# Eight wide then eight narrow products in the FFN up stage, and the last value-and-gate unit behind the first sparse head's scores

## The chip, the cores and the metric

The kernel runs on one NeuronCore of one Trainium2 chip. The metric is the device time of one execution in microseconds (us), lower is better. Three runs of the kernel before took 1211.58, 1211.7 and 1215.43 us; the median is 1211.7 us. The profile is of one further execution, of 1215.52 us, whose span from the first to the last instruction is 1213.6 us.

## The reference, cut to what matters

Two blocks are computed one after the other on 256 tokens of width 1024, in fp32. The first has a latent attention, a feed-forward stage (FFN), a differential attention and a second FFN. The second has an FFN, a mixed stage (sparse attention of eight heads beside a gated recurrence of four heads) and a last FFN. Of these the change touches the four FFNs and the mixed stage:

```python
def conv_ffn(x, w_up, conv_w, conv_b, w_down):      # FFN 0 and 1, hidden 2816
    u = x @ w_up
    ...                                             # three taps along the tokens
    g, val = c[..., :FFN_HIDDEN], c[..., FFN_HIDDEN:]
    return (jax.nn.gelu(g) * val) @ w_down

def swiglu(x, w_gu, w_down):                        # FFN 2 and 3, hidden 2752
    gate, up = jnp.split(x @ w_gu, 2, axis=-1)
    return (jax.nn.silu(gate) * up) @ w_down

def hybrid_mixer(h, w_in, ...):
    parts = jnp.split(h @ w_in, IN_SPLITS, axis=-1)
    nq, k_c, v_c, k_s, v_s, k_w, v_w, gl, hq, hf, hi, hg = parts
    o_nsa = nsa_group(nq, k_c, v_c, k_s, v_s, k_w, v_w, gl, ...)
    o_hg = hgrn2_group(hq, hf, hi, hg, lower_bound, hg_norm)
    return jnp.concatenate([o_nsa, o_hg], axis=-1) @ w_out

# the end of hgrn2_group
o = o * lax.rsqrt(jnp.mean(o * o, axis=-1, keepdims=True) + EPS) * out_norm
o = o.reshape(B, S, HG_WIDTH) * jax.nn.silu(g_in)
```

## The kernel before, in words

Each fp32 operand of a large product is split in two: a rounded high part (`hi`, made by ScalarE, named ACT) and the remainder (`lo`, made by VectorE, named DVE). TensorE (PE) then multiplies hi by hi, hi by lo and lo by hi. Weights come in units of 128 x 2048 elements by the SP queue's DMAs into `raw_u`, two slots; ACT writes `hi_u`, DVE `lo_u`, and PE takes a unit when both are done. Nothing schedules by cost: each of the five engines has its own list, written out by hand, and waits on named semaphores where it needs another engine.

An FFN has 22 tiles of 128 hidden columns. For tile t, PE does `up(t)`, and between two of them `down(t-2)`, twelve products of 512 columns (lines 595 to 597). In `up`, for the gate (s = 0) and the value (s = 1) and for each of eight slices k of the input, PE does a pair (`mm_beside`, lines 601 and 602): a wide product of 512 columns with the high weights as stationary operand, against the high and low input side by side, and a narrow product of 256 columns with the low weights against the high input. The narrow one adds into the second half of the same PSUM bank. So a full tile has 16 pairs, wide and narrow in turn. Tiles 2 to 19 are in a hardware loop. The first tile of an FFN goes over k outside and s inside, since it waits for each slice of the input; the last tile of FFN 2 and 3 has only 64 hidden columns and does gate and value in one series of 8 pairs.

In the mixed stage, `mix()`, PE's order around the change is: `values_and_gates(0)` and `(1)`, the four transposes of `c_h`, `values_and_gates(2)`, the small products of the compressed keys and values (lines 1116 and 1120, which end in semaphore `c_kv`), `values_and_gates(3)`, and then the loop over the heads. One `values_and_gates(i)` is one weight unit, `U_HI + i`, with 24 products of 512 columns into PSUM banks 0 to 3; after the fourth, banks 0 and 2 hold the values of the recurrence, which DVE copies to `h_v` (line 2069), and banks 1 and 3 its gates, to which ACT applies SiLU into `h_g` (line 1621); GpSimd (POOL) multiplies these by the norm's gain (line 583). In step i of the head loop PE does `scores(i)` into banks 4 to 7 (lines 1132 to 1136), `level(i-1, 1)` (line 1178), `values(i-2)` (lines 1160 to 1164), `turn(i-1)` (line 1150, into banks 0 and 1) and `level(i, 0)` (line 1178, into bank 3). In step 0 it waits before `level(0, 0)` for `h_ready`, `h_v_out` and `h_g_out`. DVE takes the maxima of the scores (lines 2118 to 2122), ACT the exponentials (line 1638), DVE the reciprocals and the scaling (lines 2104 to 2111), and DVE also takes each level (line 2079) and updates the queries with the decay (lines 2086 and 2094); POOL updates the keys (`hgrn`, lines 541 and 545).

## Time and profile before

| | |
|---|---|
| median of three runs | 1211.7 us (1211.58 to 1215.43) |
| profiled execution | 1215.52 us |
| its span | 1213.6 us |
| mean granted TensorE clock in it | 0.991 |
| PE busy | 1170.0 us (96%), 6627 products |
| DVE busy | 809.6 us (67%) |
| ACT busy | 695.9 us (57%) |
| POOL busy | 66.4 us (5%) |
| HBM read and written | 192.84 MB and 1.05 MB, 160 GB/s over the span |
| chain of waits that ends last | PE 85%, DVE 6%, ACT 4%, DMA 2%, issue 1%, POOL 1%, SP's queue 1% |

"Busy" is the time in which at least one instruction of the engine runs. Products overlap each other in the array: one of 512 columns is shown with about 0.4 us though the next starts after less, so PE's pace is read from the distance of the starts and not from the durations. PEld is the load of a product's stationary operand, which overlaps the product before it. The granted clock of PE is 1.00 at 2.4 GHz and 0.50 at 1.2 GHz.

### The profile page before, as it was taken

Reading aid. Unit: us, or ns where it says so; the run is one execution under the profiler, and the core shown is the slowest. Engines: PE = TensorE matmul, PEld = TensorE weight load, DVE = VectorE, ACT = ScalarE, POOL = GpSimd, SP = SyncE. Lnnn points to the kernel's source line nnn. Section 1 sums busy time; section 2 is a strip of 40 time slices with the busy share of each in tenths; the row PEclk is TensorE's granted clock in tenths of the full one; section 3 lists DMA queues with packets and bytes.
Section 4 is the critical chain, followed back from the end, with each engine's and each line's share of the span. In section 5 each row is a group of like instructions: output and inputs, shape, how many; then the busy total and the mean of one; then the engine's idle time right before and its main releaser. Section 6 shows DMA issues by size and latency. Waiting matters only on the chain.

```text
span 1213.6 us, 19122 instructions
## 1 busy us (share of the span) xinstructions
PE 1170.0 (96%) x6627; PEld 990.7 (82%) x6641; DVE 809.6 (67%) x1169; ACT 695.9 (57%) x1175; POOL 66.4 (5%) x98
## 2 busy tenths in 40 slices
PE   9999999999899989999999999999988999999997
PEld 7976788888799867888886888887887877888885
DVE  5855788887656558888878555556656655665554
ACT  5455666665556547666656554545565545555543
POOL 0201000000200020000002000000000220000000
PEclk9999999999899999999999999999999999999999
DMA  7514666666343436666654666644674015767661
GB/s 225 180 56 125 184 204 191 195 175 203 111 140 132 148 115 179 203 182 203 184 163 139 207 184 181 205 122 131 184 236 139 1 36 168 200 175 201 182 165 60
DMA packets 241056, 194.55 MB, mean 160 GB/s; under 512 B 11214, under 2 KB 223792, under 8 KB 241008
## 3 DMA queue, kind: packets, MB, share of 16 engines
q1 hardware_dynamic: 240928, 193.88, 53.4%
q8 instruction: 30, 0.49, 0.2%
q14 instruction: 18, 0.15, 0.0%
q10 hardware_dynamic: 80, 0.03, 0.0%
HBM read 192.84 MB, written 1.05 MB: 160 GB/s over the span
## 4 chain that ended last, share of the span: by engine, by line
PE 85%; DVE 6%; ACT 4%; DMA 2%; issue 1%; POOL 1%; SPq 1%; POOLq 0%; ACTq 0%; DVEq 0%
PE psum L601 26%; PE psum L602 13%; PE psum L595 12%; PE psum L596 12%; PE psum L597 12%; DVE lo_u L1701 1%; PE psum L1178 1%; DMA raw_u<-in_cmp_v_w 1%; ACT hi_u L1273 1%; ACT hi_u L1276 1%; DVE lo_u L1718 1%; DMA raw_u<-in_diff_w_qkv 1%; PE psum L937 1%; PE psum L1150 1%; DVE normed L1735 1%
## 5 line engine op out<-in xcount | busy, mean ns | idle before, releaser
L601 PE MATMUL psum<-act_hl,hi_u 128*128 128x512 f32 x1392 | 495.9, 399 | 4.5 <-DVE lo_u L1718 3.2
L602 PE MATMUL psum<-act_hl,lo_u 128*128 128x256 f32 x1392 | 390.3, 280 | 0.0
L601 PEld LDWEIGHTS psum<-act_hl,hi_u 128*128 128x128 f32 x1392 | 261.5, 188 | 70.8 <-issue 7.1
L1718 DVE TENSOR_TENSOR lo_u<-raw_u,hi_u 128x2048 fp32r<-128x2048 f32 x109 | 249.8, 2291 | 93.6 <-ACT hi_u L1276 57.5
L602 PEld LDWEIGHTS psum<-act_hl,lo_u 128*128 128x128 f32 x1392 | 262.8, 189 | 3.1
L1346 ACT ACTIVATE arena<-psum 128x256 f32<-128x256 f32 x174 | 66.1, 380 | 166.9 <-PE psum L602 166.8
L1783 DVE TENSOR_TENSOR arena<-psum,arena 128x256 f32<-128x256 f32 x174 | 73.6, 423 | 110.2 <-ACT arena L1346 110.0
L1282 ACT ACTIVATE hi_u<-raw_u 128x2048 fp32r<-128x2048 f32 x72 | 137.3, 1907 | 8.5 <-DMA raw_u<-in_ffn_w_gu 8.5
L595 PE MATMUL psum<-hi_d,hid_hi 128*128 128x512 f32 (+1 forms) x352 | 138.8, 394 | 0.1
L596 PE MATMUL psum<-lo_d,hid_hi 128*128 128x512 f32 (+1 forms) x352 | 137.9, 392 | 0.0
L597 PE MATMUL psum<-hi_d,hid_lo 128*128 128x512 f32 (+1 forms) x352 | 137.0, 389 | 0.0
L1793 DVE SCALAR_TENSOR_TENSOR arena<-arena,vecs 128x255 f32<-128x255 f32 x176 | 85.1, 483 | 42.4 <-ACT arena L1354 31.4
L1723 DVE TENSOR_TENSOR lo_d<-raw_d,hi_d 128x1024 fp32r<-128x1024 f32 x88 | 106.8, 1217 | 8.3 <-ACT hi_d L1291 8.3
L595 PE MATMUL psum<-act_hl,hi_u 128*128 128x256 f32 (+1 forms) x320 | 93.3, 291 | 6.0 <-DVE lo_u L1701 5.6
L1291 ACT ACTIVATE hi_d<-raw_d 128x1024 fp32r<-128x1024 f32 x88 | 91.6, 1045 | 0.0
L596 PE MATMUL psum<-act_hl,hi_u 128*128 128x256 f32 (+1 forms) x320 | 90.9, 284 | 0.0
L597 PE MATMUL psum<-act_hl,lo_u 128*128 128x256 f32 (+1 forms) x320 | 90.9, 284 | 0.0
L1701 DVE TENSOR_TENSOR lo_u<-raw_u,hi_u 128x1024 fp32r<-128x1024 f32 (+4 forms) x62 | 65.5, 1086 | 34.2 <-ACT hi_u L1273 34.0
L1273 ACT ACTIVATE hi_u<-raw_u 128x1024 fp32r<-128x1024 f32 (+4 forms) x62 | 55.7, 944 | 55.8 <-PE psum L597 37.6
L595 PEld LDWEIGHTS psum<-hi_d,hid_hi 128*128 128x128 f32 (+1 forms) x352 | 66.0, 188 | 18.1 <-issue 3.0
L1276 ACT ACTIVATE hi_u<-raw_u 128x2048 fp32r<-128x2048 f32 x37 | 70.6, 1909 | 16.7 <-PE psum L597 12.2
L1354 ACT ACTIVATE arena<-arena,vecs 128x256 f32<-128x256 f32 x88 | 53.0, 602 | 44.8 <-DVE arena L1783 44.1
(249 smaller groups left out, 1673.7 us busy)
## 6 DMA issues: line engine op xcount, KB each, us to landing
raw_u<-in_ffn_w_up SPq DMA_DIRECT2D x88, 512.0 KB, 5.6
raw_d<-in_ffn_w_down SPq DMA_DIRECT2D x86, 512.0 KB, 3.6
raw_u<-in_ffn_w_gu SPq DMA_DIRECT2D x84, 512.0 KB, 5.6
raw_u<-in_diff_w_qkv SPq DMA_DIRECT2D x24, 512.0 KB, 4.6
raw_u<-in_w_in SPq DMA_DIRECT2D x24, 512.0 KB, 4.3
raw_u<-in_mla_w_o SPq DMA_DIRECT2D x8, 512.0 KB, 3.7
raw_u<-in_diff_w_o SPq DMA_DIRECT2D x8, 512.0 KB, 3.7
raw_u<-in_w_out SPq DMA_DIRECT2D x8, 512.0 KB, 4.1
```

Source lines behind the costliest of these rows:

```text
L595: pe.matmul(o, s_hi, m_hi, start=start, stop=False)
L596: pe.matmul(o, s_hi, m_lo, start=False, stop=False)
L597: return pe.matmul(o, s_lo, m_hi, start=False, stop=stop)
L601: pe.matmul(psum[0:n, bank, :], s_hi, m_hl.rearrange("p a t -> p (a t)"), start=start, stop=False)
L602: return pe.matmul(psum[0:n, bank, SEQ:], s_lo, m_hl[:, 0, :], start=False, stop=stop)
L1276: act.activation(unit_view(hi_u, u), unit_view(raw_u, u), ACT.Copy).then_inc(S("hi_u_done"), 1)
L1282: act.activation(u_slot(hi_u, u0), u_slot(raw_u, u0), ACT.Copy).then_inc(S("hi_u_done"), 1)
L1291: act.activation(hi_d[:, d_slot(d) if b is None else d % 2, :], raw_d[:, d % 2, :], ACT.Copy)\
L1701: dve.tensor_tensor(v[0][:, r], v[1][:, r], v[2][:, r].bitcast(F32), ALU.subtract)\
L1718: dve.tensor_tensor(v[0], v[1], v[2].bitcast(F32), ALU.subtract).then_inc(S("lo_u_done"), 1)
L1723: dve.tensor_tensor(lo_d[:, slot, :], raw_d[:, d % 2, :], hi_d[:, slot, :].bitcast(F32), ALU.subtract).then_inc(S("lo_d_done"), 1)
L1793: dve.scalar_tensor_tensor(buf[0:n, slot, o], up_sum[0:n, slot, part, x], vecs[0:n, bass.ds(w, 1)], buf[0:n, slot, o], ALU.mult, ALU.add). ...
```

## The change

Two things change. The helper `up` of the FFN does a tile's products, for gate and value each, as eight wide ones and then eight narrow ones; the first tile and the last narrow tile of FFN 2 and 3 keep the pairs. In the mixed stage one after another of `values_and_gates(1)`, `(2)` and `(3)` moves one place down the list of PE, the last of them behind `scores(0)`; ACT's `split_u(U_HI + 3)` moves behind its copy of `c_ht`; ACT copies the gates out of PSUM in head step 0 and applies SiLU to them in step 8 in one instruction; DVE takes the maxima of head 0 before its split of the next unit and not in the loop; and POOL's product with the gain moves behind `hgrn()`.

```diff
@@ pool @@
+            hgrn()
             gate = h_g.rearrange("p t (h d) -> p (t h) d", h=HGH)
-            pool.wait_ge(S("h_g_out"), 2)
+            pool.wait_ge(S("h_k_upd"), 7)
+            pool.wait_ge(S("h_g_out"), 1)
             pool.tensor_tensor(gate, gate, hgain[:].unsqueeze(1).broadcast_to([P, 8, P]), ALU.mult)\
                 .then_inc(S("h_g_gained"), 1)
-            hgrn()
+            pool.wait_ge(S("h_g_gained"), 1)
             root("hgrn", 0, 0, 8, P, "h_sums", 1).then_inc(S("rstd"), 1)
@@ tensor: ffn, up @@
-                    for s, k in order:
-                        if first and s == 0:
-                            pe.wait_ge(S("act_lo"), 8 * i + k + 1)
-                        hi, lo = views[s]
-                        mm = mm_beside(4 + 2 * slot + s, n, hi[:, k, :], lo[:, k, :], act_hl[:, k],
-                                       k == 0, k == KC - 1)
-                        if k == KC - 1:
-                            mm.then_inc(S("gate_up" if s == 0 else "used_u"), 1)
+                    if first:
...
+                        return
+                    for s, (hi, lo) in enumerate(views):
+                        o = psum[0:n, 4 + 2 * slot + s, :]
+                        for k in range(KC):
+                            pe.matmul(o, hi[:, k, :], act_hl[:, k].rearrange("p a t -> p (a t)"),
+                                      start=k == 0, stop=False)
+                        for k in range(KC):
+                            mm = pe.matmul(o[:, SEQ:], lo[:, k, :], act_hl[:, k, 0, :], start=False, stop=k == KC - 1)
+                        mm.then_inc(S("gate_up" if s == 0 else "used_u"), 1)
@@ tensor: mix @@
                 values_and_gates(0)
-                values_and_gates(1)
...
                 mm.then_inc(S("c_h_tr"), 1)
-                values_and_gates(2)
+                values_and_gates(1)
...
                 mm.then_inc(S("c_kv"), 1)
-                values_and_gates(3)
+                values_and_gates(2)
...
                     if i == 0:
+                        values_and_gates(3)
 
                         pe.wait_ge(S("h_ready"), 1)
                         pe.wait_ge(S("h_v_out"), 2)
-                        pe.wait_ge(S("h_g_out"), 2)
+                        pe.wait_ge(S("h_g_copied"), 2)
@@ scalar: mix @@
                 split_u(U_HI + 2)
-                split_u(U_HI + 3)
                 act.wait_ge(S("c_h_tr"), 1)
                 act.activation(c_ht, psum[:, 4, 0:120].rearrange("p (a b) -> p a b", a=4), ACT.Copy)\
                     .then_inc(S("c_ht_out"), 1)
+                split_u(U_HI + 3)
...
                 split_u(U_HI + 4)
-                for t in range(TT):
-                    act.wait_ge(S("used_u"), U_HI + 4)
-                    act.activation(h_g[:, t, :], psum[:, 1 + 2 * t, :], ACT.Silu).then_inc(S("h_g_out"), 1)
...
+                    if i == 0:
+                        for t in range(TT):
+                            act.wait_ge(S("used_u"), U_HI + 4)
+                            act.activation(h_g[:, t, :], psum[:, 1 + 2 * t, :], ACT.Copy).then_inc(S("h_g_copied"), 1)
+                    if i == H:
+                        act.wait_ge(S("h_g_copied"), 2)
+                        act.activation(h_g, h_g, ACT.Silu).then_inc(S("h_g_out"), 1)
@@ vector: mix @@
+                def maxima(i):
+                    dve.wait_ge(S("n_scores"), i + 1)
...
+                maxima(0)
                 split_u(U_HI + 4)
...
-                    if i < H:
-                        dve.wait_ge(S("n_scores"), i + 1)
...
+                    if 0 < i < H:
+                        maxima(i)
```

On PE, the end of the second tile of an FFN and the start of the looped tiles, before. `L601` is the wide and `L602` the narrow product; `L755` and `L709` are the loop's own instructions.

```order
L602 MATMUL psum<-act_hl,lo_u 128x256
L755 UNCONDITIONAL_BRANCH
L755 ISA
L709 ISA
L601 MATMUL psum<-act_hl,hi_u 128x512
L602 MATMUL psum<-act_hl,lo_u 128x256
L601 MATMUL psum<-act_hl,hi_u 128x512
```

The same place now; `L738` is the wide, `L741` the narrow product, and `L597` is the first of the down products.

```order
L741 MATMUL psum<-act_hl,lo_u 128x256 x8
L767 UNCONDITIONAL_BRANCH
L767 ISA
L711 ISA
L738 MATMUL psum<-act_hl,hi_u 128x512 x8
L741 MATMUL psum<-act_hl,lo_u 128x256 x8
L738 MATMUL psum<-act_hl,hi_u 128x512 x8
L741 MATMUL psum<-act_hl,lo_u 128x256 x8
L747 REGISTER_ALU
L597 MATMUL psum<-hi_d,hid_hi 128x512
```

The number of products is the same; the change between wide and narrow comes four times in a tile and not thirty-two times.

On PE in the mixed stage, the end of `values_and_gates(3)`, `scores(0)` (`L1132` to `L1136`), `level(0, 0)` (`L1178`) and the start of `scores(1)`, before:

```order
L596 MATMUL psum<-lo_u,act_hl 128x512
L597 MATMUL psum<-hi_u,act_hl 128x512
L1132 MATMUL psum<-causal_b,slopes 128x414 x2
L1133 MATMUL psum<-arena 128x143
L1134 MATMUL psum<-arena 128x128
L1135 MATMUL psum<-arena 128x271
L1136 MATMUL psum<-arena 128x256
L1178 MATMUL psum<-arena 128x128 x4
L1132 MATMUL psum<-causal_b,slopes 128x414 x2
```

Now, first the end of `values_and_gates(2)`, `scores(0)` (`L1143` to `L1147`) and the first products of `values_and_gates(3)`:

```order
L598 MATMUL psum<-lo_u,act_hl 128x512
L599 MATMUL psum<-hi_u,act_hl 128x512
L1143 MATMUL psum<-causal_b,slopes 128x414 x2
L1144 MATMUL psum<-arena 128x143
L1145 MATMUL psum<-arena 128x128
L1146 MATMUL psum<-arena 128x271
L1147 MATMUL psum<-arena 128x256
L597 MATMUL psum<-hi_u,act_hl 128x512
L598 MATMUL psum<-lo_u,act_hl 128x512
```

And the end of the unit's 24 products, `level(0, 0)` (`L1189`) and the start of `scores(1)`:

```order
L598 MATMUL psum<-lo_u,act_hl 128x512
L599 MATMUL psum<-hi_u,act_hl 128x512
L1189 MATMUL psum<-arena 128x128 x4
L1143 MATMUL psum<-causal_b,slopes 128x414 x2
L1144 MATMUL psum<-arena 128x143
```

Nothing stands any longer between the unit's last product and `level(0, 0)`, whose waits are for the copies out of the unit's banks.

On ACT between the copies of the compressed keys and values and the exponentials of head 0, before; `L1276` is the split of unit `U_HI + 4`, `L1621` the SiLU of the gates:

```order
L1616 ACTIVATE arena<-psum 15x128
L1276 ACTIVATE hi_u<-raw_u 128x2048
L1621 ACT_TABLE_LOAD
L1621 ACTIVATE arena<-psum 128x512 x2
L1638 ACT_TABLE_LOAD
L1638 ACTIVATE arena,soft<-psum,soft 128x15 x2
```

Now; `L1288` is the split, `L1647` the exponentials, `L1653` the copy of the gates:

```order
L1628 ACTIVATE arena<-psum 15x128
L1288 ACTIVATE hi_u<-raw_u 128x2048
L1647 ACT_TABLE_LOAD
L1647 ACTIVATE arena,soft<-psum,soft 128x15 x2
L1647 ACTIVATE arena,soft<-psum,soft 128x128
L1647 ACTIVATE arena,soft<-psum,soft 128x256
L1647 ACTIVATE arena,soft<-psum,soft 128x128
L1647 ACTIVATE arena,soft<-psum,soft 128x256
L1653 ACTIVATE arena<-psum 128x512 x2
```

One table load is gone here, and the gates leave PSUM behind the exponentials of head 0. The SiLU now stands in step 8, with a table load of its own, ahead of the copy of the last turned head (`L1666`):

```order
L1637 ACTIVATE arena<-arena,soft 128x128
L1637 ACTIVATE arena<-arena,soft 128x256
L1656 ACT_TABLE_LOAD
L1656 ACTIVATE arena<-arena 128x1024
L1666 ACTIVATE normed<-psum 128x1024
```

The table load that FFN 3 had at its first SiLU is gone, so over the kernel there is one load fewer.

## Rows read from the trace of the kernel before

**Rows 1.** Page, part 1: busy us (share of the span) and instructions.
```profile
PE 1170.0 (96%) x6627; PEld 990.7 (82%) x6641; DVE 809.6 (67%) x1169; ACT 695.9 (57%) x1175; POOL 66.4 (5%) x98
```

**Rows 2.** Windows, looped part of FFN 1: us; PE, PEld, DVE, ACT, POOL; clock; DMA; GB/s.
```profile
470.00:630.00 160.00, 160.00 (x841) 136.40 (x840) 132.49 (x197) 104.14 (x157) 0.00 (x0) 1.00 0.64 190
```

**Rows 3.** Page, part 5: weight loads of the wide products, xcount | busy us, mean ns | idle.
```profile
L601 PEld LDWEIGHTS psum<-act_hl,hi_u 128*128 128x128 f32 x1392 | 261.5, 188 | 70.8 <-issue 7.1
```

**Rows 4.** Timeline of PE, FFN 0: start us, duration us; twelve pairs apart.
```profile
199.91 0.40 PE L601 MATMUL psum<-act_hl,hi_u 128*128 128x512 f32 x1
...
204.15 0.40 PE L601 MATMUL psum<-act_hl,hi_u 128*128 128x512 f32 x1
```

**Rows 5.** Timeline of PE, down products of 512 columns; eight starts apart.
```profile
205.43 0.39 PE L596 MATMUL psum<-lo_d,hid_hi 128*128 128x512 f32 x1
...
207.25 0.39 PE L601 MATMUL psum<-act_hl,hi_u 128*128 128x512 f32 x1
```

**Rows 6.** Timeline of PE, three other trains: 10, 7 and 11 starts apart.
```profile
362.75 0.28 PE L596 MATMUL psum<-act_hl,hi_u 128*128 128x256 f32 x1
...
363.94 0.28 PE L597 MATMUL psum<-act_hl,lo_u 128*128 128x256 f32 x1
...
903.39 0.28 PE L1082 MATMUL psum<-lo_u,hi_d 128*30 128x256 f32 x1
...
904.21 0.28 PE L1083 MATMUL psum<-hi_u,hi_d 128*62 128x256 f32 x1
...
905.43 0.40 PE L596 MATMUL psum<-lo_u,act_hl 128*128 128x512 f32 x1
...
907.97 0.39 PE L595 MATMUL psum<-hi_u,act_hl 128*128 128x512 f32 x1
```

**Rows 7.** Timeline of PE, mixed stage; in brackets the idle time before and who ended it.
```profile
911.15 0.47 PE L595 MATMUL psum<-hi_u,act_hl 128*128 128x512 f32 x1 [0.30 <-DVE lo_u L1718]
...
929.75 0.52 PE L1132 MATMUL psum<-causal_b,slopes 128*128 128x414 bf16 x2
...
931.47 1.05 PE L1178 MATMUL psum<-arena 128*128 128x128 f32 x8
932.36 0.51 PE L1132 MATMUL psum<-causal_b,slopes 128*128 128x414 bf16 x2
...
939.22 2.08 PE L1178 MATMUL psum<-arena 128*128 128x128 f32 x8 [1.63 <-DVE arena L2086]
...
948.59 1.06 PE L1178 MATMUL psum<-arena 128*128 128x128 f32 x8
...
954.98 1.06 PE L1178 MATMUL psum<-arena 128*128 128x128 f32 x8
```

**Rows 8.** Busy time by window around `level(1, 0)`; columns as in Rows 2.
```profile
934.95:938.35 3.40, 1.24 (x10) 0.86 (x8) 3.13 (x11) 1.85 (x11) 0.00 (x0) 1.00 0.00 0
938.40:945.10 6.70, 5.88 (x22) 5.20 (x23) 2.97 (x10) 3.01 (x10) 0.00 (x0) 0.50 0.00 0
```

**Rows 9.** Timeline of DVE, mixed stage.
```profile
929.95 1.29 DVE L2069 COPY arena<-psum 128x512 f32<-128x512 f32 x2 [0.59 <-PE psum L597]
...
935.15 0.19 DVE L2104 RECIPROCAL soft<-soft 128x6 f32<-128x6 f32 x1 [1.65 <-ACT arena L1638]
...
994.53 1.22 DVE L2137 TENSOR_REDUCE st<-arena 128x8 f32<-128x1024 f32 x1 [1.93 <-ACT arena L1658]
```

**Rows 10.** Timeline of ACT, mixed stage.
```profile
908.69 1.28 ACT L1606 ACT_TABLE_LOAD   x1
909.99 0.72 ACT L1606 ACTIVATE normed<-normed 30x256 f32<-30x256 f32 x2
...
982.66 0.80 ACT L1628 ACTIVATE arena<-arena,soft 128x128 f32<-128x128 f32 x2 [0.90 <-DVE soft L2107]
986.51 1.02 ACT L1650 ACTIVATE normed<-psum 128x1024 f32<-128x1024 f32 x1 [3.04 <-PE psum L1150]
```

**Rows 11.** Timeline of POOL, mixed stage.
```profile
931.11 2.36 POOL L583 TENSOR_TENSOR arena<-arena,hgain 128x1024 f32<-128x1024 f32 x1 [95.52 <-ACT arena L1621]
```

26 lines of the change are left out of this document (17 added, 9 removed).

## The prediction

> **What bounds the kernel now.** I read the page's first part, then windows and PE's starts in the FFNs, then the three engines' timelines in the mixed stage. The first part shows PE busy for 96% of the span, DVE for 67% [rows 1]. In the looped part of FFN 1, the FFN in which DVE has most to do, PE is busy in 160 of 160 us at full clock, DVE in 132.5, ACT in 104.1 [rows 2]. The reader is to see that nothing but PE's own pace sets the time of an FFN, and that DVE has 17% to spare before it does. So in the FFNs the question is how far apart products start. Twelve pairs of a wide and a narrow product take 204.15 - 199.91 = 4.24 us, 353.3 ns a pair [rows 4]. The down products, all of 512 columns, start (207.25 - 205.43)/8 = 227.5 ns apart [rows 5]. Products of 256 columns behind each other start (363.94 - 362.75)/10 = 119.0 ns apart [rows 6]. The sum of the two is 346.5 ns: a pair costs 6.8 ns more than its parts cost in trains of their own size.
>
> In the mixed stage PE does wait. It stands from the end of `turn(0)` until 939.22, 1.63 us, for DVE's update of the queries [rows 7], and of the 3.40 us before 938.35 it is busy in 1.24 only. Right behind, from 938.40 to 945.10, its clock is granted at 0.50, 1.2 GHz [rows 8].
>
> **The FFNs, part by part.** In a group of eight pairs the change makes seven wide-to-wide and seven narrow-to-narrow steps out of fourteen steps between wide and narrow; one wide-to-narrow and one narrow-to-wide step stay, together one pair. The gain is 7 x (353.3 - 227.5 - 119.0) = 7 x 6.8 = 47.6 ns a group. There are 1392 pairs [rows 3]. The first tiles keep theirs (4 x 16 = 64), so do the last ones of FFN 2 and 3 (2 x 8 = 16); 1312 are left, 164 groups. 164 x 47.6 ns = 7.8 us. All of it lies on the path, since PE is never idle there.
>
> No trace shows a train of these very operands, so the term has two bounds. Against the gain: elsewhere 512-column products with weights as moving operand start (907.97 - 905.43)/11 = 230.9 ns apart just behind a wait [rows 6]; 7 x 3.4 x 164 = 3.9 us. For more gain: the 256-column products of the compression start (904.21 - 903.39)/7 = 117.1 ns apart [rows 6]; 7 x 8.7 x 164 = 10.0 us. I take 7.8, since the train of rows 5 is a loop in steady state and runs in the same tiles.
>
> On a pair the Trainium skill speaks against the change. The page "TensorE: Matmul & The Clock Gate", section "Back-to-back issue gap", gives a warm gap of N/2.4 + 2.5 ns for each product by itself, whatever stands beside it. By that rule a pair would cost an estimated 215.8 + 109.2 = 325.0 ns in either order and the FFN term would be 0. The trace does not agree: 353.3 ns a pair.
>
> PE's faster pace asks DVE for the same work in 2% less time; its 17% of slack covers that. With that cover gone PE would wait for `lo_u`, and the term would shrink to nothing.
>
> **The mixed stage, part by part.** (a) Before, PE waits 0.30 us for `lo_u` ahead of `values_and_gates(1)`, until 911.15 [rows 7]. Now the four transposes stand there and fill it: 0.3 us less. (b) `scores(0)` took 931.47 - 929.75 = 1.72 us [rows 7] and lay between the last unit and `level(0, 0)`; DVE's two copies out of PSUM, 1.29 us from 929.95 [rows 9], ran beside it. Now the unit comes last, the copies begin at 929.95 + 1.72 - 0.3 = 931.4 and end at 932.7, and PE has nothing to do meanwhile. This is a new wait: behind it on PE are `level(0, 0)`, `scores(1)` and all of the head loop, and it lets `level(0, 0)` start at 932.7, 1.2 us later than at 931.47. (c) But head 0's maxima and exponentials are now made beside the unit's products. Before, DVE's reciprocal waited for them until 935.15 [rows 9]. Now it waits for `level(0, 0)`, 0.9 us long by its rows (931.47 to 932.36), and DVE's take of the level, an estimated 0.8 us: 0.65 for 128 x 512 elements out of PSUM, which is half of the 1.29 us of rows 9, and 0.15 for the semaphore: 932.7 + 0.9 + 0.8 = 934.4. From the reciprocal on DVE's list is what it was: probabilities, maxima of head 1, the second level, the update of the queries, and with that `level(1, 0)`, which PE waits for. `scores(1)` is done at 932.7 + 0.9 + 1.7 = 935.3, in time for the maxima. So `level(1, 0)` comes 0.75 us sooner than 939.22, I take 0.8 for (a) to (c) together. The bounds: 1.2 us lost, if the exponentials' head start is worth nothing; 1.8 gained, if the wait of 1.63 us goes whole with a little of (a).
>
> (d) The clock. `level(1, 0)` to `level(2, 0)` took 948.59 - 939.22 = 9.37 us, the same stretch one head later 954.98 - 948.59 = 6.39 us [rows 7]; 2.98 us is what half the clock cost. Now PE is idle 1.3 us before 932.7, has 4 us of work, and is idle about 1.3 us again: nowhere is it as sparse as in the 1.24 of 3.40 us of rows 8. I expect the clock to stay at 1.00 and the 3.0 us to be saved in this execution. From none to all of it are the bounds.
>
> (e) ACT's SiLU moves to step 8, between its scaling that ends at 982.66 + 0.80 = 983.46 and the copy at 986.51, which waits 3.04 us for PE [rows 10]. A table load of 1.28 us and 1.02 us for 128 x 1024 elements [rows 10] end at 985.8: hidden, 0.7 us to spare; if not hidden, what is over delays `values(7)`. The Trainium skill has a dearer switch: "ScalarE: Activation LUTs", section "What ACT_TABLE_LOAD costs", adds a drain of 1.38 us to each load. By it the estimate is 987.1, 0.6 us too late. In the trace a load starts at 908.69 and the next activation at 909.99, so it is 1.3 us with nothing behind it [rows 10]. (f) POOL's product with the gain, 2.36 us [rows 11], moves from an idle stretch to behind the SiLU, to about 988.2; DVE asks for it only ahead of the sums at 994.53 [rows 9]. Cost nothing, 6 us of cover. (g) ACT's other moved steps, `split_u(U_HI + 3)` behind the copy of `c_ht` and one table load fewer, lie in waits of ACT; no DMA moves past another on SP's queue, and what its loads wait for is done as early as before. Nothing.
>
> **The sum.** Against the profiled execution: 1215.5 - 7.8 - 0.8 - 3.0 = 1203.9 us. That execution is at the slow end of the runs: 3.8 us over the median of 1211.7, and two of three timed runs are at 1211.6. A half clock somewhere that those two did not have is of that size, so I do not count the 3.0 us against the median: 1211.7 - 8.6 = 1203.1, and both ways meet. If the timed runs had the half clock in the mixed stage too, it is 1200.1. I predict 1203.2 us.
>
> **Rivals.** (1) The clock falls all the same. For it: two new idle stretches of 1.3 us lie 4 us apart where there were 1.4 and 1.63 with one turn between. Against it: the work between them is four times as long. Price 3.0 us: 1206.1. (2) Mixing sizes is not what costs the 6.8 ns; it is in each product of this kind, with these operands and one bank for all of a group. For it: the trains of rows 5 and 6 use other operands, and those of rows 5 change the bank after three. Against it: the train of 119.0 ns in rows 6 is made of all three kinds of product. Then the FFNs give nothing, and the time is 1211.7 - 0.8 = 1210.9, no change. (3) Slower: the weight load becomes the bound in the narrow train. A load is 188 ns long [rows 3], a narrow product's own step 119. Behind a wide product a load is covered; behind a narrow one it may not be. It decides where a narrow-to-narrow step passes 119.0 + 6.8 = 125.8 ns. At the full 188 ns, 7 x 62 x 164 = 71 us are lost: 1211.7 + 71 - 0.8 = 1282. Against it: the same loads of 128 x 128 stand behind 256 columns in rows 6, and the step is 119. (4) PE's gain is given back as waits for DVE in FFN 0 and 1, where it is 83% busy: half of the 7.8 us goes, 1207.0.
>
> **How the numbers follow.** The forecast has 0.66 (own range 1200 to 1206), rival 1 has 0.12, rival 4 0.06, rival 2 0.11, rival 3 0.03, and 0.02 are left for a gain of up to 10.0 + 1.8 + 3.0 us, 1197. A change under 0.3%, 3.6 us, can't be told from none here. Faster than 1208.1 are the forecast, rivals 1 and 4 and the rest: 0.86. Within 1208.1 and 1215.3 is rival 2: 0.11. Slower 0.03. The range of 8 in 10 leaves out rivals 2 and 3: from 1199 (7.8 or a little more in the FFNs, and half clocks gone) to 1209 (3.9 in the FFNs, rival 1 or the 1.2 us lost).
>
> **What would show it.** In the FFNs: wide starts near 227.5 and narrow ones near 119 ns apart in a full tile; 353 ns a pair still would prove rival 2, over 126 ns between narrow ones rival 3, idle rows of PE behind `lo_u` rival 4. In the mixed stage: an idle time of some 1.3 us of PE, ended by DVE's copies, before `level(0, 0)`; `level(1, 0)` to `level(2, 0)` in 6.4 us at clock 1.00; ACT's copy of the last turned head still ended by PE. The prediction is wrong if the sum of the FFNs' spans is shorter by under 3.9 or over 10.0 us.

## The result, and the profile after

The changed kernel takes 1205.95 us, the median of five runs (1202.85 to 1208.17), where the kernel before takes 1212.64 us in five runs beside them (1211.58 to 1215.43). The medians are 6.7 us apart; the ratio is 0.9934 with a 95% interval of 0.9919 to 0.9949, which is 8.0 us (6.2 to 9.8) of 1212.64. 1203.2 us was predicted, in a range of 1199 to 1209. The profiled execution took 1208.17 us with a span of 1206.3 us and a mean granted clock of 0.992. The five runs follow that clock: 1208.17, 1207.6 and 1205.95 us at 0.992 to 0.993, 1202.85 and 1203.13 us at 0.998.

The page's first part of the kernel after, columns as in [rows 1], and from its fifth part the wide products, their weight loads and the loads of the narrow ones (xcount | busy us, mean ns | idle us before them):

```profile
PE 1163.0 (96%) x6641; PEld 991.5 (82%) x6641; DVE 808.6 (67%) x1169; ACT 695.9 (58%) x1175; POOL 66.4 (6%) x98
...
L738 PE MATMUL psum<-act_hl,hi_u 128*128 128x512 f32 x1312 | 327.6, 392 | 3.2 <-DVE lo_u L1734 3.2
...
L738 PEld LDWEIGHTS psum<-act_hl,hi_u 128*128 128x128 f32 x1312 | 240.8, 188 | 50.5 <-issue 3.8
L741 PEld LDWEIGHTS psum<-act_hl,lo_u 128*128 128x128 f32 x1312 | 179.0, 190 | 12.8
```

PE is busy for 7.0 us less than in [rows 1], at the same 96% of the span, and no other engine's busy time moves by more than 1.0 us. What the change brings is therefore a faster pace of PE, in the main, and not fewer waits. The 1312 wide products are the ones the prediction counted.

The timeline of PE in FFN 0 shows one full tile and the start of the next (start us, duration us, xcount):

```profile
197.93 1.98 PE L738 MATMUL psum<-act_hl,hi_u 128*128 128x512 f32 x8
199.75 1.11 PE L741 MATMUL psum<-act_hl,lo_u 128*128 128x256 f32 x8
200.70 2.00 PE L738 MATMUL psum<-act_hl,hi_u 128*128 128x512 f32 x8
202.54 1.11 PE L741 MATMUL psum<-act_hl,lo_u 128*128 128x256 f32 x8
203.49 0.40 PE L597 MATMUL psum<-hi_d,hid_hi 128*128 128x512 f32 x1
...
206.24 1.98 PE L738 MATMUL psum<-act_hl,hi_u 128*128 128x512 f32 x8
```

The up part of a tile takes 203.49 - 197.93 = 5.56 us; the down products still take 2.75. The same part before, its first two wide products and the first down product behind it:

```profile
198.86 0.39 PE L601 MATMUL psum<-act_hl,hi_u 128*128 128x512 f32 x1
...
199.20 0.40 PE L601 MATMUL psum<-act_hl,hi_u 128*128 128x512 f32 x1
...
204.50 0.40 PE L595 MATMUL psum<-hi_d,hid_hi 128*128 128x512 f32 x1
```

It took 204.50 - 198.86 = 5.64 us. A tile takes 206.24 - 197.93 = 8.31 us. Averaged over the 72 looped tiles a tile is 8.387 us before and 8.307 us after, in all four FFNs: 80 ns a tile, 40 ns a group. The gate's wide train takes 199.75 - 197.93 = 1.82 us, 227 ns a product, but the value's, which stands behind narrow products, 202.54 - 200.70 = 1.84 us. Eight narrow ones take 0.95 us, 119 ns each.

Windows of the kernel after, columns as in [rows 2]: the looped part of FFN 1, the two stretches around the one half clock of the mixed stage, and the one behind `level(1, 0)`:

```profile
470.00:630.00 160.00, 159.93 (x846) 137.64 (x845) 132.64 (x199) 105.25 (x158) 0.00 (x0) 1.00 0.65 193
890.50:893.90 3.40, 0.84 (x8) 0.85 (x8) 2.61 (x3) 2.32 (x4) 0.00 (x0) 1.00 0.17 54
894.00:897.30 3.30, 3.30 (x18) 3.30 (x17) 2.01 (x2) 3.06 (x5) 0.00 (x0) 0.50 0.99 320
...
936.40:943.10 6.70, 6.69 (x46) 5.71 (x47) 4.62 (x12) 4.42 (x18) 2.85 (x2) 1.00 0.00 0
```

In the same 160 us the profile shows 846 products of PE where it showed 841 [rows 2], still without idle time worth a name, and DVE's busy time grows by 0.15 us. The stretch behind `level(1, 0)`, which had a clock of 0.50 [rows 8], now has 1.00. But 894.00 to 897.30 has 0.50, where before it was 1.00, behind 3.40 us of which PE was busy in 0.84.

The timeline of PE in the mixed stage, kernel after; in brackets the idle time before and who ended it:

```profile
893.08 0.36 PE L597 MATMUL psum<-act_hl,hi_u 128*128 128x256 f32 x1 [2.56 <-DVE lo_u L1717]
...
902.30 0.47 PE L597 MATMUL psum<-hi_u,act_hl 128*128 128x512 f32 x1
...
908.77 0.40 PE L1118 MATMUL psum<-ident,normed 30*128 30x30 f32 x4 [0.76 <-ACT normed L1618]
...
930.51 1.13 PE L1189 MATMUL psum<-arena 128*128 128x128 f32 x8 [1.43 <-DVE arena L2099]
...
936.41 1.16 PE L1189 MATMUL psum<-arena 128*128 128x128 f32 x8 [1.30 <-DVE arena L2116]
...
942.90 1.06 PE L1189 MATMUL psum<-arena 128*128 128x128 f32 x8
```

From the first product of `values_and_gates(0)` (902.30) to `level(1, 0)` (936.41) is 34.11 us. For the same stretch before, the row of its start in PE's timeline of the kernel before is

```profile
905.13 0.47 PE L595 MATMUL psum<-hi_u,act_hl 128*128 128x512 f32 x1 [0.63 <-DVE lo_u L1701]
```

and with 939.22 of [rows 7] it is 34.09 us. Behind it `level(1, 0)` to `level(2, 0)` takes 942.90 - 936.41 = 6.49 us where it took 9.37 [rows 7].

Where the 7.35 us between the two profiled executions went: the four FFNs, each from its first up to its last down product, take 185.65, 185.78, 181.67 and 181.52 us where they took 187.27, 187.18, 183.16 and 183.16, 6.15 us together; the mixed stage, from the last product of FFN 2 to the first of FFN 3, takes 190.61 where it took 191.73, 1.12 us; 0.1 us is elsewhere. The 80 ns of 82 tiles would be 6.6 us, so some of it does not reach the spans: from the first product to the first looped tile, FFN 1 takes 22.39 us after and 22.32 before, FFN 2 20.68 and 20.73, so their second tiles give nothing. And not all of the 6.15 us is PE's pace. The table load that FFN 3 no longer has at its first SiLU took 1.28 us of ACT there before:

```profile
1028.17 1.28 ACT L1369 ACT_TABLE_LOAD   x1
...
1031.98 2.29 DVE L1718 TENSOR_TENSOR lo_u<-raw_u,hi_u 128x2048 fp32r<-128x2048 f32 x1 [0.85 <-ACT hi_u L1276]
```

The split of the next weight unit stood behind it, and PE's first looped tile began at 1034.52, 0.25 us behind the end of DVE's part of it (1031.98 + 2.29), in `e1_ffn_only` also 0.25 us behind it. Without the load DVE is done 0.9 us ahead of that product. The same FFN is then 0.38 us shorter with the old `up` (183.16 and, in `e2_mix_only`, 182.78 us) and 0.23 with the new one (181.75 in `e1_ffn_only`, 181.52 here).

### The profile page after: what moved, and what is told of

Same layout as the page of the kernel before. It is cut to its first block and busy times, and to the rows that moved or that the text cites. A ratio compares the mean times of both kernels' runs of the same rounds, so it can differ in the third digit from the quotient of the medians.

```text
span 1206.3 us, 19137 instructions
## 1 busy us (share of the span) xinstructions
PE 1163.0 (96%) x6641; PEld 991.5 (82%) x6641; DVE 808.6 (67%) x1169; ACT 695.9 (58%) x1175; POOL 66.4 (6%) x98
## 5 line engine op out<-in xcount | busy, mean ns | idle before, releaser
L738 PE MATMUL psum<-act_hl,hi_u 128*128 128x512 f32 x1312 | 327.6, 392 | 3.2 <-DVE lo_u L1734 3.2
L738 PEld LDWEIGHTS psum<-act_hl,hi_u 128*128 128x128 f32 x1312 | 240.8, 188 | 50.5 <-issue 3.8
L741 PEld LDWEIGHTS psum<-act_hl,lo_u 128*128 128x128 f32 x1312 | 179.0, 190 | 12.8
L741 PE MATMUL psum<-act_hl,lo_u 128*128 128x256 f32 x1312 | 182.9, 282 | 0.0
L597 PE MATMUL psum<-hi_d,hid_hi 128*128 128x512 f32 (+1 forms) x352 | 138.8, 394 | 0.1
L597 PE MATMUL psum<-act_hl,hi_u 128*128 128x256 f32 (+1 forms) x320 | 93.3, 292 | 7.3 <-DVE lo_u L1717 7.0
L1288 ACT ACTIVATE hi_u<-raw_u 128x2048 fp32r<-128x2048 f32 x37 | 70.6, 1909 | 21.2 <-PE psum L599 16.5
L597 PEld LDWEIGHTS psum<-hi_d,hid_hi 128*128 128x128 f32 (+1 forms) x352 | 66.4, 189 | 14.6 <-issue 3.1
```

The lines of the kernel that those rows point to most:

```text
L597: pe.matmul(o, s_hi, m_hi, start=start, stop=False)
L738: pe.matmul(o, hi[:, k, :], act_hl[:, k].rearrange("p a t -> p (a t)"), start=k == 0, stop=False)
L741: mm = pe.matmul(o[:, SEQ:], lo[:, k, :], act_hl[:, k, 0, :], start=False, stop=k == KC - 1)
L1288: act.activation(unit_view(hi_u, u), unit_view(raw_u, u), ACT.Copy).then_inc(S("hi_u_done"), 1)
```

## The experiments

Ratios are against the kernel before on the same chip; e1 to e4 share one chip, e5 to e8 another, e9 to e12 a third. Microseconds given for a ratio are its difference from 1, of the median of before. "Tile" is the mean distance between the starts of two tiles of the FFNs.

### The two parts alone, and the whole again

`e1_ffn_only` is the kernel before with the new `up`, and nothing of the mixed stage:

```diff
-                    for s, k in order:
...
-                        mm = mm_beside(4 + 2 * slot + s, n, hi[:, k, :], lo[:, k, :], act_hl[:, k],
-                                       k == 0, k == KC - 1)
+                    for s, (hi, lo) in enumerate(views):
+                        for k in range(KC):
+                            pe.matmul(o, hi[:, k, :], act_hl[:, k].rearrange("p a t -> p (a t)"),
+                                      start=k == 0, stop=False)
+                        for k in range(KC):
+                            mm = pe.matmul(o[:, SEQ:], lo[:, k, :], act_hl[:, k, 0, :], start=False, stop=k == KC - 1)
```

> The kernel before with the FFN grouping alone; the mixed stage is the old one. Theory (PE's steps): a full tile's 32 up products last 5.56 us and not 5.64 us, 82 tiles give 6.5 to 7 us, so the ratio to before is 0.9945 +- 0.0015. Rival (the clock): the gain of the whole change is mostly that of fewer half-clock stretches in the mixed stage, and grouping alone gives under 3 us (ratio over 0.9975).

Measured: 1207.91 us in six runs, 1212.24 us for the kernel before in seventeen, ratio 0.9962 (0.9948 to 0.9976), 4.6 us (2.9 to 6.3). That is less than the 6.5 to 7 us expected, though the tile is 8.307 us, as in the whole. In its trace PE's timeline at the second head's level reads:

```profile
936.27 1.16 PE L1188 MATMUL psum<-arena 128*128 128x128 f32 x8 [1.62 <-DVE arena L2096]
...
942.76 1.06 PE L1188 MATMUL psum<-arena 128*128 128x128 f32 x8
```

This is the order of before in the mixed stage, with the same wait as in [rows 7] (1.62 us for 1.63), and yet the stretch behind it takes 6.49 us: no half clock. So that half clock does not come with the order of before. This execution had one of 3.4 us from 644.7 us instead, at the start of FFN 2, and that FFN takes 183.21 us where the changed kernel's takes 181.67; the other three take 185.60, 185.61 and 181.75. That is 1.5 us less gain than the tiles give, and it brings the four FFNs' sum to 4.6 us, the size of the ratio's gain. Four of its six runs have a clock of 0.992. Whether the new order makes a half clock there more frequent stays open: the changed kernel shows none in its two profiles, two experiments below (`e8_group2`, `e10_scores1`) show one. The stretch ahead of it can be as sparse without it: of the 3.40 us before 643.7 PE is busy in 1.48 in `e4_after_again`, where the clock stays at 1.00, and of the 3.40 us before 644.6 in 1.60 here.

`e2_mix_only` is the complement: the changed kernel with the old `up`.

```diff
-                    for s, (hi, lo) in enumerate(views):
...
+                    for s, k in order:
...
+                        mm = mm_beside(4 + 2 * slot + s, n, hi[:, k, :], lo[:, k, :], act_hl[:, k],
+                                       k == 0, k == KC - 1)
```

> The kernel before with the mixed-stage part alone; the FFNs keep the pairs. Theory: level(1, 0) starts 0.8 us sooner, and the half clock that stood behind it is gone, which is worth up to 3 us in executions that had it: ratio to before 0.9975 to 0.9993, between 1 and 3 us. Rival: PE's new wait of 1.4 us ahead of level(0, 0) and a half clock at another place take it all back: ratio 1.000 or over.

Measured: 1210.55 us in twelve runs, ratio 0.9984 (0.9973 to 0.9995), 1.9 us (0.6 to 3.3). Its timeline of PE:

```profile
938.25 1.16 PE L1179 MATMUL psum<-arena 128*128 128x128 f32 x8 [1.31 <-DVE arena L2106]
...
944.74 1.06 PE L1179 MATMUL psum<-arena 128*128 128x128 f32 x8
```

This is within the 1 to 3 us expected. Neither this profile nor that of `e1_ffn_only` has a half clock in the mixed stage, which takes 187.84 us here and 188.53 there in the old order. With the 0.38 us of FFN 3's table load above, that makes 1.1 us in the traces.

`e4_after_again` is the changed kernel, unaltered, on this chip.

> The changed kernel once more, as the base for the others on the same chip: ratio to before 0.9934 +- 0.0015. If what it saves is the sum of its parts, it saves what grouping alone and the mixed stage alone save together; if PE's earlier arrival at the mixed stage turns into waits for the compression weights' DMAs, it saves up to 1.5 us less than the two together.

Measured: 1204.43 us, ratio 0.9941 (0.9925 to 0.9956). The savings of the parts, 0.38% and 0.16%, add up to 0.54%, and the whole saves 0.59% (0.44 to 0.75): within the intervals the two parts add up. Its profiled execution had no half clock in the mixed stage, which took 187.49 us, 3.1 less than in the first profile of the same kernel. Part of that is waiting and not clock: at the place where PE waited 2.56 us for a weight unit it waits 1.20 here. From the first product of `values_and_gates(0)` to `level(1, 0)` it was 932.83 - 899.28 = 33.55 us. The four transposes waited only 0.18 us for `normed`.

### What a pair costs

`e3_wides_first` puts the wide products of gate and value together, then the narrow ones:

```diff
-                    for s, (hi, lo) in enumerate(views):
-                        o = psum[0:n, 4 + 2 * slot + s, :]
+                    outs = [psum[0:n, 4 + 2 * slot + s, :] for s in range(2)]
+                    for o, (hi, lo) in zip(outs, views):
                         for k in range(KC):
                             pe.matmul(o, hi[:, k, :], act_hl[:, k].rearrange("p a t -> p (a t)"),
                                       start=k == 0, stop=False)
+                    for s, (o, (hi, lo)) in enumerate(zip(outs, views)):
                         for k in range(KC):
                             mm = pe.matmul(o[:, SEQ:], lo[:, k, :], act_hl[:, k, 0, :], start=False, stop=k == KC - 1)
```

> The changed kernel, with all 16 wide products of a tile (gate and value) ahead of its 16 narrow ones. Backlog theory: narrow products leave something that the next wide ones pay (233, 236, 228, 232 and 231 ns instead of 226.7 behind the gate's narrow train), so with no wide train behind a narrow one inside the tile its up products last 5.54 us instead of 5.56 us, 1.5 us less over the kernel than the changed kernel. Rival: the gate's sum is ready 1.8 us later, ACT and DVE fall behind, and PE waits; the same time or slower than the changed kernel.

Measured: 1207.02 us, ratio 0.9949 (0.9935 to 0.9964), not better than the changed kernel although a tile is shorter, 8.287 us. So the theory holds for the tile, and the rival for the time. PE's timeline, one tile of FFN 0, and the end of that FFN:

```profile
198.28 3.79 PE L738 MATMUL psum<-act_hl,hi_u 128*128 128x512 f32 x16
201.90 2.08 PE L742 MATMUL psum<-act_hl,lo_u 128*128 128x256 f32 x16
...
206.56 0.61 PE L738 MATMUL psum<-act_hl,hi_u 128*128 128x512 f32 x2
...
300.74 0.47 PE L597 MATMUL psum<-hi_d,hid_hi 128*128 128x512 f32 x1 [1.17 <-DVE hid_lo L1817]
```

All sixteen wide steps are now 227 ns (3.62 us). FFN 2 and 3 gain 0.4 us each over the changed kernel (181.29 and 181.12 us). FFN 0 and 1 lose 1.1 and 1.0 (186.78 and 186.75), since the gate's sum is complete only when its narrow products are, near the end of the up part, and the gelu with its three taps behind it is late for the last down products: PE idles 1.17 us.

`e9_wides_tail` keeps the changed kernel's order in the last tile, to spare it that wait:

```diff
+                    if isinstance(t, int) and t == FT - 1:
+                        for s, (hi, lo) in enumerate(views):
...
+                        return
+                    outs = [psum[0:n, 4 + 2 * slot + s, :] for s in range(2)]
+                    for o, (hi, lo) in zip(outs, views):
...
```

> All 16 wide products first in every full tile but the last of an FFN, which keeps eight and eight. Theory (the late gate sum cost e3 its gain only where no later tile covers it): the tile period stays at 8.287 us, the idle stretches of 1.17 us at the end of FFN 0 and 1 are gone, and the kernel is 1 to 1.6 us faster than the changed kernel: ratio to before 0.9925 to 0.9935. Rival (the late sum costs in every tile through ACT and DVE): no faster than the changed kernel, 0.994 or over.

Measured: 1207.63 us, where the kernel before took 1213.86, ratio 0.9953 (0.994 to 0.9966). The tile is 8.287 us, but the idle time stays:

```profile
289.93 1.98 PE L739 MATMUL psum<-act_hl,hi_u 128*128 128x512 f32 x8
...
301.24 0.47 PE L597 MATMUL psum<-hi_d,hid_hi 128*128 128x512 f32 x1 [1.15 <-DVE hid_lo L1827]
```

The timeline of DVE tells where it is from. In the same kernel, the last weight remainder of FFN 0's down part and the last hidden tile:

```profile
293.28 2.36 DVE L1750 TENSOR_TENSOR lo_d<-raw_d,hi_d 128x1024 fp32r<-128x1024 f32 x2 [1.43 <-ACT hi_d L1314]
...
300.67 0.43 DVE L1827 TENSOR_TENSOR hid_lo<-arena,hid_hi 128x256 fp32r<-128x256 f32 x1 [0.48 <-ACT hid_hi L1402]
```

The same two in DVE's timeline of the changed kernel (its FFN 0 starts 1.01 us sooner):

```profile
291.24 2.36 DVE L1739 TENSOR_TENSOR lo_d<-raw_d,hi_d 128x1024 fp32r<-128x1024 f32 x2 [1.44 <-ACT hi_d L1303]
...
298.63 0.42 DVE L1816 TENSOR_TENSOR hid_lo<-arena,hid_hi 128x256 fp32r<-128x256 f32 x1 [0.48 <-ACT hid_hi L1391]
```

DVE's list, and with it ACT's, stands 2.04 us later than in the changed kernel (293.28 for 291.24), PE's last tile only 0.6 (289.93 for 289.31). ACT's timelines show that the tile before made them late: ACT copies its gate sum out of PSUM 4.78 us into that tile (286.42, the tile begins at 281.64), and in the changed kernel 2.96 us into it (283.96 and 281.00). The last tile's own order does not mend it. What I expected of this kernel fell. A version with the wides first in FFN 2 and 3 alone was not tried; from their spans (181.67 + 181.52 - 181.29 - 181.12) it would give an estimated 0.8 us.

The other four take one theory each of why a pair costs 353.3 ns. `e5_shifted` alternates as before, but the narrow product of slice k stands behind the wide one of slice k + 1, so that no slice of the input is read twice in a row:

```diff
+                        for k in range(KC + 1):
+                            if k < KC:
+                                pe.matmul(o, hi[:, k, :], act_hl[:, k].rearrange("p a t -> p (a t)"),
+                                          start=k == 0, stop=False)
+                            if k:
+                                mm = pe.matmul(o[:, SEQ:], lo[:, k - 1, :], act_hl[:, k - 1, 0, :],
+                                               start=False, stop=k == KC)
```

> The changed kernel with wide and narrow products of a full tile in turn again, but the narrow product of slice k stands behind the wide one of slice k + 1, so no narrow product reads the slice of the input that the product ahead of it has just read. Size theory (the alternation of sizes costs it): a tile's up part lasts 5.64 us, its period 8.39 us, as before the change. Rival (a second read of the same slice costs it): 16 x 346.7 ns = 5.55 us, period 8.30 us, as grouped.

PE's timeline, the starts of two tiles of FFN 0:

```profile
198.84 0.62 PE L739 MATMUL psum<-act_hl,hi_u 128*128 128x512 f32 x2
...
207.20 0.62 PE L739 MATMUL psum<-act_hl,hi_u 128*128 128x512 f32 x2
```

Measured: a tile takes 207.20 - 198.84 = 8.36 us, 27 ns less than before and 53 more than the changed kernel, nearer to the 8.39 of the theory that the sizes cost it than to the 8.30 of the other. Each series begins with two wide products and ends with two narrow ones here, so even the 27 ns need not be the slice: rereading explains at most a third of the 80. (One execution, 1206.88 us, with a clock of 0.999; the kernel before took 1212.72 on this chip.)

`e6_pairs288` gives the narrow product 288 columns in the old order; the 32 further columns add what does not belong there, so it does not compute the reference. If a pair has a floor of its own, for two weight loads say, it stays at 353 ns; if time goes by columns it becomes 366.6.

```diff
+                            x = act_hl[:, k].rearrange("p a t -> p (a t)")
+                            pe.matmul(o, hi[:, k, :], x, start=k == 0, stop=False)
+                            mm = pe.matmul(o[:, 224:512], lo[:, k, :], x[:, 0:288], start=False, stop=k == KC - 1)
```

> The changed kernel with the pairs of before, where each narrow product of a full tile has 288 columns instead of 256 (it adds 32 columns that don't belong there, so the output is not the reference's). Floor theory: a narrow product's step is held at a floor of some 120 ns by its weight load and not by its 256 columns (113 ns), and what it falls short of the floor is paid by the wide one; with 288 columns (an estimated 126.7 ns at 32 / 2.4 = 13.3 ns more) nothing is short, and a pair lasts the same 353.3 ns, the up part 5.64 us. Rival: the cost belongs to the change of size, and 32 more columns come on top: a pair of 366.7 ns, an up part of 5.85 us, and with 1312 pairs the kernel is 17 us slower than before.

PE's timeline, the wide products of one tile of FFN 0 (its first, its ninth and its last) and the first of the next tile:

```profile
200.04 0.39 PE L739 MATMUL psum<-act_hl,hi_u 128*128 128x512 f32 x1
...
202.94 0.39 PE L739 MATMUL psum<-act_hl,hi_u 128*128 128x512 f32 x1
...
205.48 0.40 PE L739 MATMUL psum<-act_hl,hi_u 128*128 128x512 f32 x1
...
208.58 0.39 PE L739 MATMUL psum<-act_hl,hi_u 128*128 128x512 f32 x1
```

Measured: (205.48 - 202.94)/7 = 362.9 ns a pair, 9.6 of the 13.3 ns that 32 columns should cost, and 208.58 - 200.04 = 8.54 us a tile (1222.35 us, one execution). A floor at 353 is ruled out, and the time does not go by columns alone either.

`e7_group4` and `e8_group2` make groups of four and of two in place of eight:

```diff
-                        for k in range(KC):
-                            pe.matmul(o, hi[:, k, :], act_hl[:, k].rearrange("p a t -> p (a t)"),
-                                      start=k == 0, stop=False)
-                        for k in range(KC):
-                            mm = pe.matmul(o[:, SEQ:], lo[:, k, :], act_hl[:, k, 0, :], start=False, stop=k == KC - 1)
+                        for k0 in range(0, KC, 4):
+                            for k in range(k0, k0 + 4):
+                                pe.matmul(o, hi[:, k, :], act_hl[:, k].rearrange("p a t -> p (a t)"),
+                                          start=k == 0, stop=False)
+                            for k in range(k0, k0 + 4):
+                                mm = pe.matmul(o[:, SEQ:], lo[:, k, :], act_hl[:, k, 0, :], start=False, stop=k == KC - 1)
```

(In `e8_group2` the two 4s are 2s.)

> The changed kernel in groups of four wide and four narrow. Floor theory: each narrow product but the first of a train has a step of 120 ns, and what one wide product behind a train has to pay does not grow much with the train: three trains of narrow ones inside the tile have wide ones behind them, so the up part lasts between 5.56 and 5.64 us, near 5.60 us. Rival (a cost at each change of size, 15 of them from narrow to wide in a tile of pairs, 6.9 ns each): 5.54 + 3 x 0.007 = 5.56 us, as grouped by eight.

PE's timeline of `e7_group4`, the starts of two tiles:

```profile
198.27 1.07 PE L739 MATMUL psum<-act_hl,hi_u 128*128 128x512 f32 x4
...
206.62 0.62 PE L739 MATMUL psum<-act_hl,hi_u 128*128 128x512 f32 x2
```

> The changed kernel in groups of two wide and two narrow. Floor theory: seven trains inside the tile with wide ones behind them, each paying more than half of what eight narrow ones leave (27 ns): 5.63 us or more, all of the gain gone. Rival (a cost at each change of size): 5.54 + 7 x 0.007 = 5.59 us.

PE's timeline of `e8_group2`, the first three groups of a tile and the start of the next:

```profile
197.87 0.62 PE L739 MATMUL psum<-act_hl,hi_u 128*128 128x512 f32 x2
198.32 0.40 PE L742 MATMUL psum<-act_hl,lo_u 128*128 128x256 f32 x2
198.55 0.63 PE L739 MATMUL psum<-act_hl,hi_u 128*128 128x512 f32 x2
...
206.16 0.61 PE L739 MATMUL psum<-act_hl,hi_u 128*128 128x512 f32 x2
```

Measured: 8.35 us a tile in groups of four, 8.29 in groups of two (1207.79 and 1206.3 us, one execution each). A fixed price for each change of size would make groups of four better than groups of two. It is the other way round. The theory of a floor under the narrow products expected 5.60 us for the up part in groups of four, which is near, and 5.63 or more in groups of two, which fell:

| group | 1 (before) | 2 | 4 | 8 (after) | 16 |
|---|---|---|---|---|---|
| tile, us | 8.387 | 8.293 | 8.353 | 8.307 | 8.287 |
| up part, us | 5.640 | 5.563 | 5.587 | 5.559 | 5.539 |

The simple theories have fallen: a floor of the pair, the column count alone, and a price per change of size. Why a pattern has its pace stays open. What is shown is that the pace belongs to the pattern, is the same in every looped tile to 1 ns, and has to be measured. One regularity can be read from the starts of the looped tiles: in trains a wide product takes 226.7 ns and a narrow one 120 (the first behind wide ones 113), and behind a train of narrow products the first five wide ones together take 27 ns more than 226.7 each, behind eight narrow ones (`after`) as behind sixteen (`e3_wides_first`); behind two (`e8_group2`) the two wide ones that follow take 16 more.

### The mixed stage and the clock

`e10_scores1` puts the scores of head 1 ahead of the wait before `level(0, 0)`, to fill the new wait of 1.43 us:

```diff
-                    if i < H:
+                    if i < H and i != 1:
                         scores(i)
                     if i == 0:
                         values_and_gates(3)
+                        scores(1)
```

> The changed kernel with scores(1) ahead of the waits that stand before level(0, 0), so PE's new idle stretch of 1.43 us holds 1.7 us of work. Theory (DVE's chain from level(0, 0) to the update of the queries sets level(1, 0)): level(0, 0) starts 0.2 to 0.3 us later, level(1, 0) too, and PE stands the longer before level(1, 0): nothing gained, ratio as the changed kernel. Rival (PE's order sets it): 1.4 us faster.

PE's timeline, `level(0, 1)` and `level(1, 0)`:

```profile
931.80 1.16 PE L1189 MATMUL psum<-arena 128*128 128x128 f32 x8 [0.87 <-DVE arena L2110]
...
935.69 1.16 PE L1189 MATMUL psum<-arena 128*128 128x128 f32 x8 [1.63 <-DVE arena L2117]
```

Measured: 1205.59 us, ratio 0.9933 (0.9919 to 0.9946), no different from the changed kernel. The first wait is filled, and what it gives comes back as a wait of 0.87 us before `level(0, 1)` and of 1.63 instead of 1.30 us before `level(1, 0)`, as expected. Both are ended by DVE. So DVE's list (copies, level, maxima, second level, update) sets `level(1, 0)`, and no order of PE's work moves it.

`e11_warm` fills idle stretches with products that compute nothing, ahead of places where half clocks had been seen: 30 in place of 19 fillers in the third entry of `WARM`, and 9 before `heads_turn(3)`.

```diff
-WARM = [(0, 4, 6)] + 4 * [(19, 3, 1)] + 2 * [(12, 3, 1)]
+WARM = [(0, 4, 6), (19, 3, 1), (30, 3, 1), (19, 3, 1), (19, 3, 1)] + 2 * [(12, 3, 1)]
 ...
+                keep_warm(9, 7)
```

> The changed kernel with 11 more idle-filling products ahead of the transposes of the differential attention's norm (30 and not 19) and 9 new ones ahead of the last heads' transposes in it. They compute nothing. Theory (the half clocks behind the two idle stretches of 2.7 to 4 us cost 3 to 4.5 us in most executions, and explain most of the spread between runs): the clock stays at 1.00 there, the median falls by 3 to 4.5 us and the spread of the runs narrows; ratio to before 0.9905 to 0.9915. Rival (other engines set the time there, so PE's clock is worth little): under 1 us.

Measured: 1204.7 us, ratio 0.993 (0.9916 to 0.9944). The granted clock of its six runs is 0.996 to 0.999, higher than the changed kernel's 0.992 to 0.998, and its longest half clock before the end of FFN 3 is 3.4 us where there were 6.8. The stage between FFN 0 and FFN 1 takes 143.56 us for 144.94. But its interval holds the changed kernel's ratio and not the 0.9905 to 0.9915 expected: if there is a gain it is under a microsecond or two. The trace shows a place where the gain can go, the mixed stage's compression, where PE waits for weight units:

```profile
882.72 2.01 ACT L1286 ACTIVATE hi_u<-raw_u 128x1024 fp32r<-128x1024 f32 x2 [4.05 <-DMA raw_u<-in_cmp_v_w]
...
886.31 0.35 PE L597 MATMUL psum<-act_hl,hi_u 128*128 128x256 f32 x1 [2.02 <-DVE lo_u L1718]
```

The mixed stage takes 189.12 us, where it took 187.49 in `e4_after_again`. The stage in front had gained 1.08 us over that kernel. So in this pair of executions the weights' DMAs take back more than the clock gave. Whether they do because PE comes sooner stays open: these waits differ between executions of one kernel too.

`e12_best` takes e9, e10 and e11 together.

```diff
+WARM = [(0, 4, 6), (19, 3, 1), (30, 3, 1), (19, 3, 1), (19, 3, 1)] + 2 * [(12, 3, 1)]
...
+                    if isinstance(t, int) and t == FT - 1:
...
+                keep_warm(9, 7)
...
+                        scores(1)
```

> e9, e10 and e11 together. Theory: the gains add, 1.5 us of e9 and 3 to 4.5 of e11, nothing of e10: ratio to before 0.989 to 0.991, some 1200 us. Rival: idle stretches that are filled in one place let the clock fall in another (in the compression's weight units, where PE waits for DMAs the longer the sooner it arrives), and no more than 2 us remain beside the changed kernel.

Measured: 1205.52 us, ratio 0.9943 (0.9927 to 0.9958). Its profiled execution has no half clock before the end of FFN 3 (mean 0.998), and it is still no faster than the changed kernel. Its span is 1202.5 us, that of `e4_after_again` 1202.7: the stage between FFN 0 and 1 gains 3.1 us (141.54 for 144.64), the four FFNs lose 1.2 (735.85 for 734.64) by the idle time of e9, and the mixed stage loses 1.6 (189.11 for 187.49), with longer waits for the compression's weights again. The rival in its expectation was no more than 2 us beside the changed kernel, from the same place, and fits. None of the versions beats the changed kernel by more than the measurement's interval.

## Why the prediction was right, point by point

**FFNs, 7.8 us predicted: the mechanism holds, the size was 6.6 by the tiles and 6.15 by the spans.** The step is the sum 7 x (353.3 - 227.5 - 119.0) = 47.6 ns a group. Measured are 40 ns a group, 80 a tile. What was mis-sized is the group before: sixteen pairs at 353.3 ns would be 5653 ns a tile, and the up part took 5640, since its first pair, behind the down products, takes 0.34 us (199.20 - 198.86) and not 0.353. The tile after came out as the sum has it, 5558 ns for its two groups and 5559 measured, but by two errors that cancel, which is luck. A wide product in a train takes 226.7 ns by the exact starts and not 227.5, 13 ns less a tile. And the price of mixing that the prediction kept, 2 x 6.8 = 14 ns a tile, is 27: nothing in the gate's group (227 and 119 ns), all of it in the value's, which stands behind narrow products, so that its wide steps fall only slowly to 227 (1.84 - 1.82 = 0.02 us more by the rows above). The down products behind the value's narrow train begin the same way; the train of [rows 5] was read in its middle, where this no longer shows. `e3_wides_first` confirms it: with one seam fewer the tile falls by another 20 ns. The rule of the Trainium skill that spoke against this term ("TensorE: Matmul & The Clock Gate", section "Back-to-back issue gap", a gap by a product's own columns, which the section calls the isolated one) is not borne out: the same 32 products of an up part take 5.64, 5.56 or 5.54 us by their order alone. Of the 6.15 us in the spans 0.2 to 0.4 are the table load of FFN 3, and `e1_ffn_only` alone gave 4.6 (2.9 to 6.3), so 6.6 us is what the tiles' pace is worth and not what the kernel got from it.

**No waits for DVE in FFN 0 and 1: right.** PE is busy in 159.93 of 160 us. (PE asks for the same work in 1% less time, 80 ns of 8387, and not in 2% as the prediction has it; that only makes its argument stronger.) How near the edge is, `e3_wides_first` and `e9_wides_tail` show: a gate's sum that comes 1.8 us later in the tile (4.78 - 2.96) costs 1.1 us at the end of each FFN.

**(a) to (c), 0.8 us predicted: 0.5 for (b) and (c) as computed, (a) wrong.** The stretch from `values_and_gates(0)` to `level(1, 0)` takes 34.09 us (before) and 34.29 us (`e1_ffn_only`, 936.27 - 901.98) in the order of before. In the new order it takes 33.3 to 34.1 us in ten profiles; 33.55 in `e4_after_again`, 33.64 in `e2_mix_only`, 34.11 in the profiled execution. The new wait before `level(0, 0)` is 1.43 us (1.3 predicted), the one before `level(1, 0)` 1.30 for 1.63, both ended by DVE as said. What was missed is in (a): the transposes fill the wait for `lo_u`, but they wait themselves for ACT's gelu into `normed`, from under 0.1 (`e7_group4`, `e8_group2`, `e9_wides_tail`, 33.3 us) to 0.76 us. Without that wait, and without the 0.30 or 0.49 us for `lo_u` in the old order, the stretch is 33.8 us before and 33.35 after: 0.45 us, which is what (b) and (c) come to in the prediction (0.75 less the 0.3 of (a)). In the profiled execution, with 0.76, nothing is left of the 0.8.

**(d) The clock, 3.0 us in the profiled execution: right at its place, not in the sum.** The stretch is 6.49 us at a clock of 1.00, as forecast. But 894.00 to 897.30 ran at 0.50. Ahead of it PE waited 2.56 us for a weight unit, where the kernel before waited 1.62 us at the same place, and was busy in 0.84 of 3.40 us. So rival 1 (the clock falls all the same) came true in that execution, at another place than it named. `e1_ffn_only` shows that [rows 8] does not belong to the old order either. Not counting the 3.0 us against the median was right: the mixed part's median gain is 1.9 us (0.6 to 3.3), and a half clock of before in every run would have made it 3.8.

**(e) and (f), SiLU and POOL at no cost: right; (g), one table load fewer at no gain: wrong by 0.2 to 0.4 us,** by the two pairs of spans of FFN 3 above. For (e) and (f), the timelines of ACT and of POOL, kernel after:

```profile
977.79 1.28 ACT L1656 ACT_TABLE_LOAD   x1
979.09 1.06 ACT L1656 ACTIVATE arena<-arena 128x1024 f32<-128x1024 f32 x1
980.82 1.02 ACT L1666 ACTIVATE normed<-psum 128x1024 f32<-128x1024 f32 x1 [0.67 <-PE psum L1161]
```

```profile
980.29 2.35 POOL L585 TENSOR_TENSOR arena<-arena,hgain 128x1024 f32<-128x1024 f32 x1 [1.28 <-ACT arena L1656]
```

ACT's next copy still waits 0.67 us for PE, 0.7 were predicted to spare. POOL is done at 982.64, and DVE's sum that needs it starts at 988.84. Between the load's start and the SiLU's are 1.30 us, so the drain of 1.38 us that the Trainium skill adds to a load ("ScalarE: Activation LUTs", section "What ACT_TABLE_LOAD costs") does not show here either.

**Rivals.** 2 (the 6.8 ns is in each product) fell with the tile of 8.307 us. 3 (slower, by the weight load of 188 ns) fell with narrow steps of 119 ns: the loads are still shown with 188 and 190 ns, and do not hold the narrow train up. 4 (given back as waits for DVE) fell with the 159.93 us.

**The sum.** 7.8 + 0.8 = 8.6 us were predicted off the median. By the traces it is 6.15 for the FFNs' spans, table load included, and 0.5 for the wait chain, 6.6 us together; 6.7 by the medians, 8.0 (6.2 to 9.8) by the ratio, were measured. The kernel before took 1212.64 us in the five runs and not the 1211.7 that the forecast started from. The forecast's own range, 1200 to 1206, just holds the 1205.95.
